# A sparse expert table built on ScalarE for one prompt tile and on VectorE for the other

## The reference, cut to what matters

```
def peer(x2d, w_pq, sub_keys, peer_u, peer_v):
    ...                                             # 8 heads x top 16 of 128 x 128 = 16384 experts
    def experts(args):
        xb, ib, gb = args
        a = jnp.einsum("thkd,td->thk", peer_u[ib], xb)
        act = jax.nn.gelu(a, approximate=False) * gb
        return jnp.einsum("thk,thkd->td", act, peer_v[ib])
```

## Time and profile before

| | before |
|---|---|
| three runs, us | 3026.33, 3040.02, 3036.27 (median 3036.27) |
| profiled execution, us | 3039.85 |
| its span, us | 3037.9 |
| busy, us: PE, DVE, ACT, POOL | 2115.3, 1926.8, 362.3, 1283.7 |
| DMA over the span | 345 GB/s, 1048.10 MB |

### The profile page before, as it was taken

One profiled execution on the slowest core, in us unless ns is written; L12 is line 12 of the kernel. 1 busy time (PEld: TensorE's weight loads), 2 busy tenths in 40 slices (PEclk: granted clock), 3 DMA queues, 4 the chain that ended last, 5 costly groups with the idle time before them and its releaser, 6 DMA issues.

```text
span 3037.9 us, 19222 instructions
## 1 busy us (share of the span) xinstructions
PE 2115.3 (70%) x6070; PEld 1071.5 (35%) x6070; DVE 1926.8 (63%) x2585; ACT 362.3 (12%) x785; POOL 1283.7 (42%) x853
## 2 busy tenths in 40 slices
PE   7999999899999897887979500000012137999996
PEld 3665444444544443333434200000011126444443
DVE  1222000286677775644655899999999999666666
ACT  1212100112222110001010100000011126000000
POOL 2000000014355444533533445688877765445444
PEclk9999999999999999999989855555555556999998
DMA  9676788759799999889979767899999997999999
GB/s 342 259 284 242 244 285 312 251 216 389 289 403 381 363 411 395 348 320 382 374 301 363 302 242 302 313 422 422 422 418 417 415 366 222 404 408 403 408 409 350
DMA packets 271603, 1048.10 MB, mean 345 GB/s; under 512 B 19872, under 2 KB 19872, under 8 KB 203296
## 3 DMA queue, kind: packets, MB, share of 16 engines
q0 software_dynamic: 113648, 696.80, 57.1%
q1 hardware_dynamic: 155168, 346.06, 31.5%
q10 hardware_dynamic: 2704, 4.21, 0.4%
HBM read 1037.55 MB, written 9.45 MB: 345 GB/s over the span
## 4 chain that ended last, share of the span: by engine, by line
DVE 20%; DMA 19%; PE 17%; POOL 7%; issue 6%; ACT 0%; POOLq 0%; DVEq 0%; SPq 0%; ACTq 0%
PE ps L565 16%; DMA yTr<-in_peer_v,fold 12%; DVE bigr L1459 9%; POOL bigr L536 5%; DMA bigr<-in_w_br_a 4%; DVE hr L1490 2%; DVE spare L1459 1%; DVE normed L1480 1%; POOL spare L536 1%; DVE pwork L1296 1%; DMA bigr<-in_w_pq 1%; DVE bigs L1394 1%; POOL yTr L546 1%; DMA bigs<-in_peer_v,idxnow 1%; DMA bigr<-in_w_out 1%
## 5 line engine op out<-in xcount | busy, mean ns | idle before, releaser
L565 PE MATMUL ps<-bigr 128*128 128x512 f32 x1920 | 850.3, 601 | 42.3 <-DMA bigr<-in_w_in 23.6
L565 PEld LDWEIGHTS ps<-bigr 128*128 128x128 f32 x1920 | 365.4, 193 | 493.8 <-issue 439.7
L1459 DVE SCALAR_TENSOR_TENSOR bigr<-bigr 128x2048 f32<-128x2048 f32 x214 | 483.5, 2287 | 13.7 <-DMA bigr<-in_peer_u,fold 13.1
L536 POOL DMA_INDIRECT bigr<-in_peer_u,fold x214 | 412.5, 1928 | 154.3 <-DVE bigr L1459 64.7
L497 POOL DMA_INDIRECT bigs<-in_peer_u,idxnow x128 | 225.8, 1764 | 591.3 <-DVE bigs L1404 555.5
L565 PE MATMUL ps<-bigr,bigs 128*128 128x512 f32 x896 | 405.8, 608 | 26.7 <-DMA bigr<-in_w_in 22.4
L1490 DVE SCALAR_TENSOR_TENSOR hr<-yTr,fold,hr 128x1024 f32<-128x1024 f32 x205 | 263.2, 1284 | 134.9 <-DMA yTr<-in_peer_v,fold 134.1
L1394 DVE SCALAR_TENSOR_TENSOR bigs<-bigs,acts 128x2048 f32<-128x2048 f32 x128 | 300.7, 2349 | 63.9 <-DMA bigs<-in_peer_v,idxnow 63.6
L1404 DVE SCALAR_TENSOR_TENSOR bigs<-bigs 128x2048 f32<-128x2048 f32 x128 | 293.0, 2289 | 71.8 <-DMA bigs<-in_peer_u,idxnow 71.0
L828 PE MATMUL ps<-normed,pwork 128*128 128x128 f32 x512 | 121.9, 414 | 278.9 <-DVE normed L1480 245.1
L546 POOL DMA_INDIRECT yTr<-in_peer_v,fold x205 | 215.6, 1052 | 227.4 <-DVE hr L1490 216.7
(11 more groups left out here) (246 smaller groups left out, 1852.2 us busy)
## 6 DMA issues: line engine op xcount, KB each, us to landing
bigr<-in_w_in SPq DMA_DIRECT2D x160, 1024.0 KB, 6.3
spare<-in_peer_v SPq DMA_DIRECT2D x96, 512.0 KB
bigr<-in_w_out SPq DMA_DIRECT2D x32, 1024.0 KB, 6.0
bigr<-in_w_pq SPq DMA_DIRECT2D x32, 1024.0 KB, 6.2
bigr<-in_w_br_a SPq DMA_DIRECT2D x16, 1024.0 KB
bigr<-in_w_br_b SPq DMA_DIRECT2D x16, 1024.0 KB, 11.1
bigr<-in_peer_v SPq DMA_DIRECT2D x32, 512.0 KB
bigr<-in_ckT_a POOLq DMA_DIRECT2D x2, 2048.0 KB, 10.5
```

The costliest lines, as they stand in the source:

```text
L536: pool.indirect_dma_start(ER.urow[k % UBUF], None, a["peer_u"][:, :], bass.IndirectOffsetOnAxis(ap=eidx[t][:, s:s + 1], axis=0)).then_inc( ...
L565: last = mm(ps[:, bank + t, :], src[:, k0 + k, t * P:(t + 1) * P], wring[:, s, k, :], start=(k0 + k == 0), stop=(k0 + k == kt - 1))
L1459: dve.scalar_tensor_tensor(ER.urow[u], ER.urow[u], 1.0, R.xn2[:, t, :], ALU.mult, ALU.mult, accum_out=rdots[:, t, s:s + 1]).then_inc(ER.u_ ...
```

## The change

ACT makes tile 0's one-hots itself. For each of a quad's four tokens it computes |column - grid| (`distances`: eight activations of 128 x 128, Abs with the column as a per-partition bias), and then relu(1 - distance) over 128 x 512, twice (`hots` on ACT). The scaling into `hot_a` and `place_table` stay as they were. DVE makes nothing for tile 0 any more. A new semaphore, `apart`, orders the two ACT steps.

For tile 1, DVE makes `hot_a` directly, one instruction per token that compares the grid with j and multiplies by the activation (two per-partition operands), and `hot_i` as before. ACT only places tile 1's tables. `hots(1, 0)` now has to wait for the turned activations (`act_placed`). Instead of one add per quad there is one add after every third quad, ten in all, and 246 adds after them.

```
-            def hots(t, q):
-
-                g = QUADS * t + q
+            def hots(q):
+
+                g = QUADS + q
                 b = g % 2
...
-                dve.tensor_tensor(hot_j[:, b, :, :], column(1), grid, ALU.is_equal).then_inc(ER.j_hot, 1)
-                dve.tensor_tensor(hot_i[:, b, :, :], column(0), grid, ALU.is_equal).then_inc(ER.i_hot, 1)
+                dve.wait_ge(ER.g_done, g - 1)
+                for n in range(QUAD):
+                    k = q * QUAD + n
+                    last = dve.tensor_scalar(hot_a[:, b, n, :], iotaP, pairT[:, 1, 1, k:k + 1], ractT[:, 1, k:k + 1],
+                                             ALU.is_equal, ALU.mult)
+                last.then_inc(ER.a_hot, 1)
+                dve.tensor_tensor(hot_i[:, b, :, :], pairT[:, 1, 0, rows_].unsqueeze(2).to_broadcast([P, QUAD, P]),
+                                  iotaP.unsqueeze(1).to_broadcast([P, QUAD, P]), ALU.is_equal).then_inc(ER.i_hot, 1)
...
-                if k >= SLOTS + TURN and k % TURN == TURN - 1:
-                    hots(0, (k - SLOTS) // TURN - 1)
-            hots(0, QUADS - 1)
             prompt_acts(1)
-            dve.wait_ge(ER.acts_ready, 2)
+            dve.wait_ge(ER.pair_placed, 2)
+            dve.wait_ge(ER.grid_made, 1)
+            dve.wait_ge(ER.a_hot, QUADS)
+            dve.wait_ge(ER.i_hot, QUADS)
+            dve.wait_ge(ER.act_placed, 2)
+            early = QUADS // 3
             for q in range(QUADS):
-                hots(1, q)
-                add_half(q)
-            for k in range(QUADS, 2 * SLOTS):
+                hots(q)
+                if q % 3 == 2:
+                    add_half(q // 3)
+            for k in range(early, 2 * SLOTS):
                 add_half(k)
```

On ACT:

```
+            def distances(q):
+
+                b = q % 2
+                if q >= 2:
+                    act.wait_ge(ER.a_hot, q - 1)
+                    act.wait_ge(ER.g_done, q - 1)
+                for w, hot in ((1, hot_j), (0, hot_i)):
+                    for n in range(QUAD):
+                        last = act.activation(hot[:, b, n, :], iotaP, ACT.Abs, scale=-1.0,
+                                              bias=pairT[:, 0, w, q * QUAD + n:q * QUAD + n + 1])
+                last.then_inc(ER.apart, 1)
+
+            def hots(q):
+
+                b = q % 2
+                act.wait_ge(ER.apart, q + 1)
+                act.activation(hot_j[:, b, :, :], hot_j[:, b, :, :], ACT.Relu, scale=-1.0, bias=1.0
+                               ).then_inc(ER.j_hot, 1)
+                act.activation(hot_i[:, b, :, :], hot_i[:, b, :, :], ACT.Relu, scale=-1.0, bias=1.0
+                               ).then_inc(ER.i_hot, 1)
+                act.wait_ge(ER.j_hot, q + 1)
...
-                scaled(t, 0)
+                    distances(0)
+                    hots(0)
                 for q in range(QUADS):
-                    if q + 1 < QUADS:
-                        scaled(t, q + 1)
+                    if t == 0 and q + 1 < QUADS:
+                        distances(q + 1)
+                        hots(q + 1)
                     place_table(t, q)
```

More of the change, by code:

```diff
@@ L184, in __init__ @@
         self.grid_made = sem("grid_made")
+        self.apart = sem("apart")
         self.j_hot = sem("j_hot")
@@ L1062, in place_pair @@
                                ACT.Copy).then_inc(ER.pair_placed, 1)
-            def scaled(t, q):
-                g = QUADS * t + q
-                act.wait_ge(ER.j_hot, g + 1)
+            def distances(q):
[16 more added lines that the diff above has]
+                act.wait_ge(ER.j_hot, q + 1)
                 for n in range(QUAD):
-                    last = act.activation(hot_a[:, g % 2, n, :], hot_j[:, g % 2, n, :], ACT.Copy,
-                                          scale=ractT[:, t, q * QUAD + n:q * QUAD + n + 1])
+                    last = act.activation(hot_a[:, b, n, :], hot_j[:, b, n, :], ACT.Copy,
+                                          scale=ractT[:, 0, q * QUAD + n:q * QUAD + n + 1])
                 last.then_inc(ER.a_hot, 1)
@@ L1091, in _ @@
                     act.wait_ge(y_stored, 16)
-                scaled(t, 0)
+                    act.wait_ge(ER.pair_placed, 1)
+                    act.wait_ge(ER.grid_made, 1)
+                    distances(0)
+                    hots(0)
                 for q in range(QUADS):
-                    if q + 1 < QUADS:
-                        scaled(t, q + 1)
+                    if t == 0 and q + 1 < QUADS:
+                        distances(q + 1)
+                        hots(q + 1)
                     place_table(t, q)
@@ L1465, in prompt_acts @@
                 dve.tensor_tensor(gates[t], rdots[:, t, :], gates[t], ALU.mult).then_inc(ER.acts_ready, 1)
-            def hots(t, q):
-                g = QUADS * t + q
+            def hots(q):
+                g = QUADS + q
                 b = g % 2
[L1471 to L1478, removed]
-                dve.tensor_tensor(hot_j[:, b, :, :], column(1), grid, ALU.is_equal).then_inc(ER.j_hot, 1)
-                dve.tensor_tensor(hot_i[:, b, :, :], column(0), grid, ALU.is_equal).then_inc(ER.i_hot, 1)
+                rows_ = slice(q * QUAD, (q + 1) * QUAD)
+                dve.wait_ge(ER.g_done, g - 1)
[6 more added lines that the diff above has]
+                                  iotaP.unsqueeze(1).to_broadcast([P, QUAD, P]), ALU.is_equal).then_inc(ER.i_hot, 1)
             def add_half(k):
@@ L1501, in _ @@
                     prompt_acts(0)
-                    dve.wait_ge(ER.pair_placed, 2)
-                    dve.wait_ge(ER.grid_made, 1)
-                if k >= SLOTS + TURN and k % TURN == TURN - 1:
-                    hots(0, (k - SLOTS) // TURN - 1)
-            hots(0, QUADS - 1)
-            prompt_acts(1)
-            dve.wait_ge(ER.acts_ready, 2)
+            prompt_acts(1)
+            dve.wait_ge(ER.pair_placed, 2)
[4 more added lines that the diff above has]
+            early = QUADS // 3
             for q in range(QUADS):
-                hots(1, q)
-                add_half(q)
-            for k in range(QUADS, 2 * SLOTS):
+                hots(q)
+                if q % 3 == 2:
+                    add_half(q // 3)
+            for k in range(early, 2 * SLOTS):
                 add_half(k)
```

## The result

| | before | changed |
|---|---|---|
| median of 6 runs, us | 3035.35 | 3054.30 |
| lowest to highest, us | 3026.33 to 3040.02 | 3048.13 to 3064.69 |
| profiled execution, us (span) | 3039.85 (3037.9) | 3064.69 (3062.7) |
| ratio to before, 95% interval | | 1.0065 [1.0046, 1.0083] |

The changed kernel is slower by 0.65%, 19 us. The two profiled executions lie 24.8 us apart; 3.3 us of that had come about before the first edited instruction (tile 0's activations start at 2170.78 before and at 2174.04 after), and is variation between executions. So from here on I count from that instruction, A0.

What follows compares the result with a forecast made beforehand. DMA engines and DVE bound the dots, DVE the table stretch, PE and DMA dense. Dense starting 23.7 us earlier and 31.9 us of adds behind it sum to +8.2 us, 3044 us; 8-in-10 range 3029 to 3059.

Steps and rivals of the forecast that it cites:

- slower rival: Tile 1's one-hot stretch on DVE: its new instructions lengthen it, +18 us, 3054 us; chance 0.28.
- likeliest case: Whole program: the forecast taken alone, 3044 us, with 3031 to 3051 us; chance 0.57.
- last dot: End of tile 1's dots: ends at 2486.0 us against 2488.8, bounds 2484.2 and 2488.9.
- seam: From last dot to tile 1's first one-hot on DVE: 1.8 us, the one-hot starting 8.0 us earlier.
- adds behind dense: After the dense stretch: 21 more adds at 1.52 us each, 31.9 us, bounds 27 and 35.
- Tile 1's quads: DVE's tile 1 one-hots: 0.207 us per scaled one-hot, 1.43 us a quad, 60 us in all, bounds 50 and 69.
- rival 1: Tile 1's quads: scaled one-hots at 0.28 us (9.4 us more) or POOL's issues holding DVE (10 us more); chance 0.28.
- two-buffer ring: Tile 1's quads: DVE may write quad q + 2 only when PE finishes q; adds some 2 us.
- The other half of rival 1: Tile 1's quads: POOL's ten gather issues of about 1 us each hold DVE, 10 us more; whole rival's chance 0.28.
- ACT hidden: ACT's tile 0 steps during the dots: 5.6 us a quad, 179 us in all, done by 2351, hidden.
- the fixed number of adds beside it: Dense stretch: adds get only DMA's leftover, so their number cannot rise; clearly above 213 would refute it.
- Faster rival: Dense stretch: adds not held by bandwidth, so the program follows dense's earlier start, -23.7 us, 3013 us; chance 0.12.

Runs made afterwards that it cites:

- e5: Changed kernel with constant 1.0 replacing the activation operand in tile 1's scaled one-hots (one per-partition operand); profile alone: four take 0.78 us, table stretch 57.6 us.
- e6: Changed kernel with adds from slot 225 on over 512 columns instead of 1024, gathers whole; profile alone: tail 41.8 us instead of 48.8.
- e7: Changed kernel with SP's first four dense blocks loaded only after the last dot; one execution: dots end 3.1 us earlier.
- e1: Kernel before with an add after every third quad of tile 1 instead of every quad, one-hots unchanged; ratio to before 1.0069.
- e3: Changed kernel with an add after every quad (32) instead of every third; ratio to before 1.0024.
- e4: Kernel before with ACT making tile 0's one-hots and 43 adds instead of 32 over tile 1's quads; ratio to before 0.9993.

## Why the prediction was right or wrong

The measured 3054.3 us lies within the range of 3029 to 3059, but at the 3054 us of the slower rival, not in the likeliest case. That it meets the rival's number is partly luck: the dearer one-hots that the rival names are about half of the 13 us that the forecast lacked, and the rest came from the last dots, the slow start of dense and the tail. The direction (slower than before) and the mechanism were the forecast's: an earlier dense stretch, paid for with adds behind it. The sizes, counted from A0:

| term | forecast | measured |
|---|---|---|
| last dot | -2.8 | -0.1 |
| seam (last dot to first one-hot) | 7.0 to 1.8 | 7.0 to 1.8 |
| table stretch | 75.6 to 60 | 75.6 to 67.4 |
| one-hots to dense | 3.2, no change | 3.2 to 2.9 |
| start of dense | -23.7 | -13.8 |
| length of dense | 439.5 | 441.7 (439.7 before) |
| adds behind dense | +31.9 | +33.2 |
| sum | +8.2 | +21.4 |

- *Tile 1's quads: the step that failed.* "I take 0.207, the row of the same kind" was the price of one per-partition operand (0.195 in e5); with two it is 0.257, just short of the 0.26 at which I had let rival 1 begin. Over 128 instructions that is 6.4 us, where rival 1 had 9.4 for its first half. With one operand the stretch is 57.6 us (e5), so the rest of the step's working held. The two-buffer ring that I had put at 2 us is not what failed: DVE waits for it 2.7 us in the changed kernel's stretch and 1.1 us in e5's.
- *The other half of rival 1*, POOL's issues holding DVE, did not happen: the four one-hots beside an issue take 1.05 us (2533.27 - 2532.22 in the changed kernel's timeline), against 1.03 without. The holding is found in the other place and the other direction: behind dense, DVE's adds hold POOL's issues (e6). The Trainium skill's sentence that I had weighed there (SBUF — State Buffer, section "SBUF: two separate sides") lets whichever starts first block the other. The trace agrees for an issue that begins under a running add; the adds that begin under a running issue take their usual 1.28 us.
- *Last dot.* I let the five v rows be the ones that come late, and the four dense blocks be in already. It was the blocks that came first, and the last dots waited; e7 shows the 3.1 us. The upper bound (2488.9 us, all blocks ahead) was the right one.
- *Seam, ACT hidden, dense's length, the fixed number of adds beside it:* as forecast, ACT even faster (5.2 us a quad instead of 5.6). Dense's first records at 1.2 GHz were not foreseen, 2 us; e6 and e7, with the same code there, have them at 2.4 GHz, so the change alone doesn't bring them.
- *Adds behind dense.* 29 adds begin there instead of 9, so 20 more, where I had 21. They come 1.69 us apart, not 1.52. The 1.67 us of the same place in the kernel before was the right row, and I had passed it over for POOL's issues; one add fewer hid about half of that.
- *Faster rival (adds not held by bandwidth):* refuted by 214 against 215 adds beside dense, and by e1.
- *The median.* The measured difference of the medians is 19 us, near the 21.4 of the profiles and 11 above the 8 forecast.

## What to carry to other kernels

Where a stretch has a full resource and a neighbour has it half idle, work moved from the half idle stretch to the full one does not vanish; count where it comes out (here behind both, at a worse rate), and look for the number at which the two ends meet. Busy time taken off an engine buys nothing while its next input comes at the DMA engines' pace (here 37 us of DVE's): look at the waits before it, at both ends of the stretch. And price an instruction by a row with the same operands, since one more per-partition operand made this one a third dearer.

## What the hardware showed that I had not expected

- A TENSOR_SCALAR of 128 x 128 in float32 takes 0.195 us with one per-partition operand and 0.257 with two (e5, changed kernel).
- An indirect gather's issue on POOL that began while a DVE add was running ended 0.81 to 0.86 us after that add's end, and so took up to 1.97 us (changed kernel, behind dense). Where no add was running at its start it took 0.94 us (e6).
- PE's granted clock was 0.50 at the start of dense in the changed kernel, e3 and e4, and 1.00 in the other eight, e6 with the same code up to there among them. PE came from the same kind of small matmuls in all; what decides it is left open.
